# Expert gather of a two-block transformer layer: two places for down rows instead of four, and two query tiles loaded ahead into the room

## The reference

```python
def block(tb):                                  # tb: 128 tokens x 2048
    qh = (tb @ w_query).reshape(P_BLOCK, P_HEADS, 2, P_DQ // 2)
    s = jnp.einsum('thpd,hpkd->thpk', qh, sub_keys).astype(jnp.float32)
    sv, si = lax.top_k(s, P_TOPK)
    cand_s = (sv[:, :, 0, :, None] + sv[:, :, 1, None, :]).reshape(P_BLOCK, P_HEADS, P_TOPK * P_TOPK)
    cand_i = (si[:, :, 0, :, None] * P_NKEYS + si[:, :, 1, None, :]).reshape(P_BLOCK, P_HEADS, P_TOPK * P_TOPK)
    best_s, best_j = lax.top_k(cand_s, P_TOPK)
    eid = jnp.take_along_axis(cand_i, best_j, axis=-1)
    g = jax.nn.softmax(best_s, axis=-1)
    act = jax.nn.gelu(jnp.einsum('thkd,td->thk', expert_down[eid], tb).astype(jnp.float32), approximate=False)
    return jnp.einsum('thk,thkd->td', (g * act).astype(tb.dtype), expert_up[eid])
```

## Time and profile before

| | |
|---|---|
| time, median of 2 runs | 3403.74 us (3403.07 to 3404.42) |
| profiled execution: time | 3401.59 us |
| its span | 3399.8 us |
| busy, of the span | PE 85%, PEld 60%, DVE 54%, ACT 34%, POOL 69% |
| gathers in the queue of GpSimd | 73728 packets, 536.90 MB |
| query tiles, chunks 0, 2 and 3, in the ring (`weight_ring<-peer_query`) | 12, 17.1 us from issue to landing (median) |
| down gathers: who waited for them | DVE, 184.1 us idle before its dots, 179.4 of it for the gather |

### The profile page before, as it was taken

The page is one execution under the profiler, slowest core; times in us unless marked ns, Lnnn a source line. Parts: engine busy times, 40 slices in busy tenths (PEclk is TensorE's granted clock), DMA queues, the critical chain, the costliest instruction groups (busy, mean ns, idle before and its releaser), DMA issues. The chain is left out here.

```text
span 3399.8 us, 30787 instructions
## 1 busy us (share of the span) xinstructions
PE 2904.0 (85%) x11248; PEld 2041.8 (60%) x11248; DVE 1824.3 (54%) x2377; ACT 1145.8 (34%) x1860; POOL 2338.9 (69%) x1120
## 2 busy tenths in 40 slices
PE   6999999999986666655656776589999999999998
PEld 2787888888753333322222322248888888888887
DVE  3577537412678777778988887751147412111122
ACT  3322456544421111111221112134455444444443
POOL 0244677588667575657776677868767698888887
PEclk8999999999988888877678887889999999999999
DMA  9999855365699999999999999985545456656554
GB/s 397 338 349 335 302 173 169 126 231 192 241 420 426 425 427 425 427 427 427 412 427 427 427 427 426 427 324 188 172 154 189 138 197 194 227 190 206 190 191 164
DMA packets 308075, 1015.86 MB, mean 299 GB/s; under 512 B 21932, under 2 KB 26640, under 8 KB 241104
## 3 DMA queue, kind: packets, MB, share of 16 engines
q1 hardware_dynamic: 231336, 475.62, 40.5%
q0 software_dynamic: 73728, 536.90, 37.5%
q10 hardware_dynamic: 2860, 1.38, 0.1%
HBM read 1009.59 MB, written 4.24 MB: 298 GB/s over the span
## 5 line engine op out<-in xcount | busy, mean ns | idle before, releaser
L729 POOL TENSOR_TENSOR block_weights_lo<-weight_ring,block_weights_hi 128x1024 fp32r<-128x1024 f32 x596 | 1444.3, 2432 | 577.7 <-ACT block_weights_hi L722 563.1
L1909 PE MATMUL banks<-up_rows,pick_diagonal 128*128 128x512 f32 x1024 | 681.3, 827 | 438.9 <-DMA up_rows<-peer_up,picked_experts 377.5
L722 ACT ACTIVATE block_weights_hi<-weight_ring 128x1024 fp32r<-128x1024 f32 x608 | 640.8, 1059 | 997.6 <-PE banks L3063 315.9
L1909 PEld LDWEIGHTS banks<-up_rows,pick_diagonal 128*128 128x128 f32 x1024 | 262.4, 269 | 826.4 <-issue 732.5
L1766 POOL DMA_INDIRECT up_rows<-peer_up,picked_experts x256 | 483.3, 1888 | 338.6 <-DVE expert_sum L2219 113.7
L2272 DVE CUSTOM_DVE_ANT_0 down_rows<-down_rows,h_tokens 128x2048 f32<-128x2048 f32 x256 | 583.7, 2291 | 184.1 <-DMA down_rows<-peer_down,picked_experts 179.4
L1758 POOL DMA_INDIRECT down_rows<-peer_down,picked_experts x256 | 405.4, 1584 | 101.3 <-issue 78.3
L2219 DVE SCALAR_TENSOR_TENSOR expert_sum<-up_rows,pick_share,expert_sum 128x2048 f32<-128x2048 f32 x125 | 293.9, 2352 | 51.4 <-ACT pick_share L2053 45.5
L2047 ACT ACTIVATE pick_gelu<-pick_dots 128x2 f32<-128x2 f32 x127 | 25.8, 203 | 834.0 <-DVE pick_dots L2272 833.7
L2497 PE MATMUL banks<-block_weights_hi,h_T_hi 128*128 128x512 f32 x688 | 272.8, 397 | 2.3 <-POOL block_weights_lo L729 2.3
L2499 PE MATMUL banks<-block_weights_hi,h_T_lo 128*128 128x512 f32 x688 | 268.3, 390 | 0.0
(11 more groups left out here) (549 smaller groups left out, 4344.5 us busy)
## 6 DMA issues: line engine op xcount, KB each, us to landing
weight_ring<-w_in SPq DMA_DIRECT2D x232, 1024.0 KB, 4.9
cond_ring<-w_ada SPq DMA_DIRECT2D x128, 512.0 KB, 6.3
weight_ring<-w_ada SPq DMA_DIRECT2D x32, 1024.0 KB, 8.6
weight_ring<-w_out SPq DMA_DIRECT2D x32, 1024.0 KB, 4.9
weight_ring<-peer_query SPq DMA_DIRECT2D x12, 1024.0 KB, 17.1
weight_ring<-w_ret_out SPq DMA_DIRECT2D x8, 1024.0 KB, 4.9
weight_ring<-w_mlstm_out SPq DMA_DIRECT2D x8, 1024.0 KB, 4.9
weight_ring<-w_mem_kv SPq DMA_DIRECT2D x8, 1024.0 KB, 11.9
```

Source lines behind the costliest of these rows:

```text
L722: act.activation(self.hi[:, self.place(slot, h)], ring.tile[:, slot, h * self.HALF:(h + 1) * self.HALF], ACT.Copy).then_inc(self.hi_ready, 1)
L729: pool.tensor_tensor(self.lo[:, at], ring.tile[:, slot, h * self.HALF:(h + 1) * self.HALF], self.hi[:, at], ALU.subtract).then_inc(ring.us ...
L1909: mm = pe.matmul(ps[:, 4 + b], diag[:, G % 2], up[:, p % ROWS, b * CG:(b + 1) * CG], start=(G % PER_TB == 0), stop=(G % PER_TB == PER_TB - ...
```

## The change

`down_rows` gets 2 places in place of 4 (`DOWN_ROWS`), with the semaphores and waits to match: down row p now waits for the dot of p-2. `up_rows` keeps 4. The room of the two places that are gone becomes `tiles_ahead`, two query tiles, which take tiles 0 and 1 of chunk 2 ahead of the gather. The other tiles of chunk 1 are no longer issued behind one common wait: tile 1 waits until the first block's weights are free, tile 0 for the second `x1_ready`, tile 2 for `h2_ready` as before; then the two new ones follow.

```diff
-        GROUPS, ROWS = TB * PICKS // 2, 4
+        GROUPS, ROWS, DOWN_ROWS = TB * PICKS // 2, 4, 2
...
+        SPARE_ROWS = ROWS - DOWN_ROWS
+        ahead = nc.alloc_sbuf_tensor_at("tiles_ahead", [P, SPARE_ROWS, TILE_K, CG], F32, offset=e.split2_at + DOWN_ROWS * D * 4)
+        early_tile = {(EARLY_CHUNK, s): tile for s, tile in enumerate(early_query)}
+        early_tile.update({(EARLY_CHUNK + 1, s): ahead[:, s] for s in range(SPARE_ROWS)})
...
-            for s, tile in sorted(enumerate(early_query), reverse=True):
-                if s == len(early_query) - 2:
+            for n, s in [(EARLY_CHUNK, s) for s in (3, 1, 0, 2)] + [(EARLY_CHUNK + 1, s) for s in range(SPARE_ROWS)]:
+                if (n, s) == (EARLY_CHUNK, 1):
+                    sp.wait_ge(e.split.free, e.split.free_after(e.split_tiles))
+                if (n, s) == (EARLY_CHUNK, 0):
+                    sp.wait_ge(x1_ready, TB)
+                if (n, s) == (EARLY_CHUNK, 2):
                     sp.wait_ge(h2_ready, TB * H_FILLS)
-                sp.dma_start(tile, k_tile(io["peer_query"][0], s, slice(EARLY_CHUNK * CG, (EARLY_CHUNK + 1) * CG))).then_inc(early_query_in[s], 16)
+                sp.dma_start(early_tile[n, s], k_tile(io["peer_query"][0], s, slice(n * CG, (n + 1) * CG))).then_inc(early_query_in[n, s], 16)
             for n in range(1, N):
                 load_tiles(sp, ring, turn_of(io["peer_query"][0], slice(n * CG, (n + 1) * CG)), base + n,
-                           skip=len(early_query) if n == EARLY_CHUNK else 0)
+                           skip=sum(1 for of, _ in early_tile if of == n))
...
-                    if p >= ROWS:
-                        pool.wait_ge(dot_done, p - ROWS + 1)
+                    if p >= DOWN_ROWS:
+                        pool.wait_ge(dot_done, p - DOWN_ROWS + 1)
                         pool.sem_inc(go, 1)
-                    pool.indirect_dma_start(down[:, p % ROWS], None, io["peer_down"][0],
-                                            bass.IndirectOffsetOnAxis(ap=expert[:, p:p + 1], axis=0)).then_inc(down_landed[p % ROWS], 16)
+                    pool.indirect_dma_start(down[:, p % DOWN_ROWS], None, io["peer_down"][0],
+                                            bass.IndirectOffsetOnAxis(ap=expert[:, p:p + 1], axis=0)).then_inc(down_landed[p % DOWN_ROWS], 16)
...
-                    if nb == 0 and n == EARLY_CHUNK and s < len(early_query):
-                        pe.wait_ge(early_query_in[s], 16)
+                    if nb == 0 and (n, s) in early_tile:
+                        pe.wait_ge(early_query_in[n, s], 16)
                         pe.sem_inc(ring.landed[s], 16)
...
-                    dve.wait_ge(down_landed[p % ROWS], in_turn(p))
+                    dve.wait_ge(down_landed[p % DOWN_ROWS], down_in_turn(p))
```

More of the change, by code:

```diff
@@ L1622, in lists_at @@
             return 8 * r - 6 if r < PEER_H else 8 * PEER_H - 6 + 6 * (r - PEER_H)
-        down, up = nc.alloc_sbuf_tensor_at("down_rows", [P, ROWS, D], F32, offset=e.split2_at), sb("up_rows", [P, ROWS, D])
+        down, up = nc.alloc_sbuf_tensor_at("down_rows", [P, DOWN_ROWS, D], F32, offset=e.split2_at), sb("up_rows", [P, ROWS, D])
         scores, acc = sb("key_scores", [P, HP, TB, PEER_K]), sb("expert_sum", [P, D])
@@ L1648, in phase_peer @@
                                     free_tile[:])
+        SPARE_ROWS = ROWS - DOWN_ROWS
+        ahead = nc.alloc_sbuf_tensor_at("tiles_ahead", [P, SPARE_ROWS, TILE_K, CG], F32, offset=e.split2_at + DOWN_ROWS * D * 4)
+        early_tile = {(EARLY_CHUNK, s): tile for s, tile in enumerate(early_query)}
+        early_tile.update({(EARLY_CHUNK + 1, s): ahead[:, s] for s in range(SPARE_ROWS)})
         gt2_row, GATE_ROW = spare_tile[0:1].rearrange("p a n -> p (a n)"), PER_TB - 8
-        query_tile = lambda n, s: early_query[s] if n == EARLY_CHUNK and s < len(early_query) else ring.tile[:, s]
+        query_tile = lambda n, s: early_tile[n, s] if (n, s) in early_tile else ring.tile[:, s]
         shift2 = lambda f: e.lat[:, f // 2, RK + f % 2 * CG:RK + (f % 2 + 1) * CG]
@@ L1668, in phase_peer @@
         h2_ready, turned, turned_out = sem("h2_ready"), sem("h2_turned"), sem("h2_turned_out")
-        early_query_in = [sem(f"early_query_in{s}") for s in range(len(early_query))]
+        early_query_in = {(n, s): sem(f"early_query_in{n}_{s}") for n, s in early_tile}
         gt2_row_in, gt2_row_spread = sem("gt2_row_in"), sem("gt2_row_spread")
@@ L1674, in phase_peer @@
         picks_ready, weights_ready, go = sem("picks_ready"), sem("weights_ready"), sem("gather_go")
-        down_landed = [sem(f"down_landed{s}") for s in range(ROWS)]
+        down_landed = [sem(f"down_landed{s}") for s in range(DOWN_ROWS)]
         up_landed = [sem(f"up_landed{s}") for s in range(ROWS)]
@@ L1704, in phase_peer @@
         in_turn = lambda p: 16 * (p // ROWS + 1)
+        down_in_turn = lambda p: 16 * (p // DOWN_ROWS + 1)
         block = ctx.enter_context(phase_block(nc, e))
@@ L2270, in _ @@
                 for p in (2 * G, 2 * G + 1):
-                    dve.wait_ge(down_landed[p % ROWS], in_turn(p))
-                    dve.tensor_tensor_reduce(down[:, p % ROWS], down[:, p % ROWS], h2[:, G // PER_TB], 1.0, 0.0, ALU.mult, ALU.add,
+                    dve.wait_ge(down_landed[p % DOWN_ROWS], down_in_turn(p))
+                    dve.tensor_tensor_reduce(down[:, p % DOWN_ROWS], down[:, p % DOWN_ROWS], h2[:, G // PER_TB], 1.0, 0.0, ALU.mult, ALU.add,
                                              dots[:, p:p + 1]).then_inc(dot_done, 1)
```

## The result

The changed kernel takes **3604.97 us** (3600.84 to 3609.09, 2 runs) against 3403.74: a ratio of 1.0598, 95% interval 1.0581 to 1.0616, 201 us more. The forecast was 3444 us with a range up to 3483. The direction was right; the forecast rise of 40 us was a fifth of what came.

The account below looks back on a forecast made before the run. The prediction took DMA transfers to bound the gather, at 427 GB/s. Losses of 23 + 14 + 7 + 6 = 50 us, less 4.9 gained and 5 for overlap, made +40 on 3403.7: 3444 us, range 3405 to 3483.

Parts of the forecast that it names:

- The lag of 4.3: Down gathers: a row lands 4.3 us behind its issue's end, taken from a span of 3.5 to 4.7.
- keep the wait: GpSimd issues starting under a VectorE add wait for its end; without this the sum would be near +17 us.
- Even row: Even down row's round: 9.84 against 9.81 us, nothing lost without lists; 14 us where lists make dots late.
- the signs named: Profile after: late-gather DMA share 0.93 to 0.96, turns 10.2 to 10.5 us, landings 5 to 7, gather ending near 2290.
- The odd row's 23 us: Turns without list work: odd down issue waits for the add, 10.35 against 9.81 us, 42 x 0.54 = 23 us lost.
- The rival of a starved turn: Gather: every turn starved, even row late from 4.55 us between issue end and landing; +79, 3483 us; chance 0.2.
- First turns: Start of the gather: VectorE starts 3 to 5 us behind landings, so down rows come later; 7 us lost.
- block 1: First turns of block 1: VectorE gates and adds the finished sum and falls behind; 6 us lost.
- routes: Turns behind the pick numbers: dots start 1.08 us late; 10 us lost, with small overlaps 14 us.
- The 4.9 us gained: Full gather stretch: two ring tile loads move ahead of it, 2 x 2.45 = 4.9 us gained.

Follow-up runs that it names:

- the rows at 1536 columns: Changed kernel with both dots over 1536 of 2048 columns; 3532.96 us, ratio 1.0387.

## Why the prediction was wrong in size

**Right, with its numbers.** The gather was bound by its transfers, and the loss passed on whole. SyncE's waits and tiles ahead went as written, and the first gather wasn't held (issued at 929.90). GpSimd's release 3.1 us behind a dot's start and the end of a held issue 0.88 us behind the instruction above it make 5.54 us for the even row; the table has 5.58. The lag of 4.3 is the median engine's 4.37 in the changed kernel and 4.29 with one place. The sum was right to keep the wait: in the changed kernel all 213 issues that begin under a dot or an add, 0.15 us or more behind its start, are held past its end, as in the 2.43 us against 0.94 in the rows at 1536 columns. The prediction took this to contradict the Trainium skill (page "SBUF — State Buffer", section "Who interferes with whom"), but read half of it. Beside the inference on descriptor writing, the section says that a VectorE instruction with two inputs in SBUF contends with a GpSimd instruction that reads SBUF. A gather takes its row numbers from `picked_experts`, which lies in SBUF, so the trace agrees with that sentence; that this read is what is held up, no run here shows.

**The step that failed** is "**Even row.** ... 2.45 + 2.21 + 0.88 + 4.3 = 9.84 against 9.81, nothing yet". The sum took the sixteen engines for one, and the lag for a number that a gather keeps whatever else is in the queue. The median engine keeps it in a short queue (4.37 us), but the row counts as landed with the last one, 6.63 us behind the issue's end. The up rows ahead don't explain it: they have landed on all engines at 2.0 us, and 2.45 more would make 4.5. So each turn takes 11.89 us in place of 10.27, tile loads and list turns included: 1.62 x 127 = 206 us from first to last turn. The forecast had +23 for the odd row and +14 for the even. By its own numbers the even row was also nearer the edge than it says: 2.45 + 2.21 + 0.88 leaves 4.27 us of the 9.81 for the lag, so that every turn's even row is late from 4.27 on and not, as in its rival, from 4.55.

**What the profile showed against the signs named.** DMA share late in the gather was 0.93, as forecast for a right sum. But turns came 11.9 us apart and not 10.2 to 10.5, down rows landed 7.2 to 9.2 us behind their issue's start (2250 to 2390 us) and not 5 to 7, and the last dot was at 2448 and not near 2290. The share agreed by luck: it hides the longer packets.

**The odd row's 23 us** was the largest term, and it didn't show: 6.5 us with the add cut short. The step that failed here is "finds the add running". In the changed kernel only 38% of the odd rows' issues are held (over 1.5 us long), since GpSimd goes on to the odd row 0.30 us behind the held even one, often just ahead of the add; the issue ends 4.38 us behind the landing at the median, and not 2.90 + 2.27 + 0.88 = 6.05. The row by itself is still late enough to cost 139 us, but beside the even row it is hidden.

**The rival of a starved turn** named the reason, "the last of the sixteen engines sets each landing", and then priced it with the first gather's 4.7 us. That gather, like the down rows of the kernel with one place, found the engines empty. No row read before could show the lag in a short queue, but the bound from above should not have been one that only empty engines give: in the kernel before, the engines' landings were already 3.6 us apart.

**First turns, block 1, routes** (7, 6 and 14 us) can't be told apart in the runs: they lie in turns that are all late now.

**The 4.9 us gained** are neither shown nor refuted. With four places and no tile ahead the time is 3401.06 us; with two places, the two tiles ahead go with 29 us less than no tile, and one tile with 4 less, within the scatter of such kernels.

**Still open** is why the engines fall apart. In the trace, a gather's 8 KB packet takes 309 ns when the queue is deep: 0.3% are over 400 ns in the kernel before, 0.6% with the shortest dots, 4.8% with only the odd dot short, 7.5% in the changed kernel and 9.7% with one place, single ones up to 2.3 us. An engine that runs dry pays with long packets when it starts again: in the changed kernel an engine's eight packets of an even row take 2.47 us where they follow directly on earlier work and 3.11 us where the engine was idle before (medians of those that can be traced back from their completion, 83%). That is too little for the last engine. In the 15 turns in which the late one's packets can be traced back without doubt, it begins them 2.25 us behind the issue's end, where the median engine begins at about 1.0, and takes 3.35 us for them. Why it begins late stays open: the trace doesn't name the engines, so it can't be said whether it is always the same one, and no run isolated it. With one place there are most long packets and the smallest spread.

No version here beats the kernel before; the best are as fast (four places, or dots that leave out work).

## What to carry to other kernels

A place in a ring of buffers is needed not until the median transfer is through but until the last of the sixteen engines is, so budget issue end to landing by the last engine with other transfers around it: here 6.6 to 7.6 us for 1 MB, against 4.3 to 4.7 us for one that finds all engines empty. Before taking a buffer away, lay out one round (landing, use, release, issue end, landing) and ask for more slack than the engines' spread (2 to 3.6 us here); a sum that came out even, 9.84 against 9.81, was a loss of 1.62 us a turn. Look at where an issue of GpSimd falls as well: one that starts 0.14 us behind a long VectorE instruction ended 0.8 us behind that instruction, and one 0.4 us sooner took 0.94 us.

## What the runs showed of the hardware that was not expected

- DMA share is not rate. It fell from 1.01 to 0.93 to 0.96 while the rate fell from 427 to 353 to 377 GB/s, since packets of engines that run dry are counted as busy for longer (mean 339 ns against 310).
- A gather into empty engines lands on all sixteen within 0.6 us, the one right behind it within 1.3; with two places for down rows they are 2 us apart and with four 3.6.
- The hold of an issue depends on which starts first, with a margin: in the changed kernel none of the 90 issues that began up to 0.9 us ahead of a dot or an add was held, of 18 that began up to 0.1 us behind its start 2 were, and all 215 that began later under it were.
- A starved kernel is also a noisy one: 3612.77 to 3651.49 us against 3399 to 3404 for the kernel before.
